# Hybrid pool and retention encoder on eight cores: first groups transposed on TensorE, last local means on GpSimd, output projection from its pool half

## The reference, cut to what matters

```python
mod = silu(c) @ ada_w + ada_b                      # conditioning
shift, scale, gate = split(mod, 3)
h = rms_norm(x, g_pre) * (1 + scale) + shift
u_pool, q, k, v, z = split(h @ w_in, ...)          # z is 2048 wide: z_pool | z_ret
y_pool = (window_mean(u_pool, w) - u_pool) @ pool_w * pool_scale   # w = 2, 4, 8, 16 by quarter of the width
y_ret = group_norm(retention_forward(q, k, v) + retention_backward(q, k, v))   # q, k rotated by position
out = (concat(y_pool, y_ret) * silu(z)) @ w_out
y = x + gate * rms_norm(out, g_post)
```

## Time and profile before

| what | value |
|---|---|
| median of 3 runs | 3066.83 us |
| profiled execution, device time | 3066.21 us |
| its span, slowest core (core 7) | 3064.6 us |
| spans of the cores | 3056.0 to 3064.6 us |
| busy, share of the span | PE 96%, DVE 78%, ACT 47%, POOL 41% |
| chain that ended last | PE 89%, DVE 4%, DMA 2%, issue 2% |

### The profile page before, as it was taken

One profiled execution on the slowest core, in us unless ns is written; L12 is line 12 of the kernel. 1 busy time (PEld: TensorE's weight loads), 2 busy tenths in 40 slices (PEclk: granted clock), 3 DMA queues, 4 the chain that ended last, 5 costly groups with the idle time before them and its releaser, 6 DMA issues.

```text
span 3064.6 us, 49885 instructions; the slowest of 8 cores (3056.0 to 3064.6 us)
## 1 busy us (share of the span) xinstructions
PE 2946.6 (96%) x17088; PEld 1475.1 (48%) x17088; DVE 2393.0 (78%) x2608; ACT 1431.7 (47%) x2381; POOL 1259.7 (41%) x968
## 2 busy tenths in 40 slices
PE   2799999999999999999799999999999999999998
PEld 1344444444444444444345555555555555555554
DVE  5488878888888878778777788777887777877774
ACT  5555556555556556553234434443444333443342
POOL 4444554554543333332134433443344433443343
PEclk9999999999999999999899999999999999999999
DMA  9966666666666655643868777777777778777774
GB/s 265 279 181 172 167 174 174 167 194 170 171 174 173 194 161 158 162 143 115 264 172 206 228 211 201 205 203 223 211 203 207 201 220 220 202 209 199 220 194 129
DMA packets 512857, 591.63 MB, mean 193 GB/s; under 512 B 329152, under 2 KB 353760, under 8 KB 505696
## 3 DMA queue, kind: packets, MB, share of 16 engines
q1 hardware_dynamic: 504352, 572.71, 66.2%
q0 software_dynamic: 3456, 10.49, 2.3%
q10 hardware_dynamic: 4800, 5.24, 0.8%
HBM read 305.70 MB, written 200.81 MB: 165 GB/s over the span
## 4 chain that ended last, share of the span: by engine, by line
PE 89%; DVE 4%; DMA 2%; issue 2%; ACT 1%; POOL 1%; ACTq 0%; SPq 0%; DVEq 0%; POOLq 0%
PE psum L848 59%; PE psum L1446 21%; PE psum L1379 4%; PE psum L1336 1%; PE psum L1412 1%; PE psum L948 1%; DMA krS<-kr 1%; ACT hT L831 1%; DMA stg<-wv 1%; ACTq L180 0%; DMA yT<-yr 0%; DVE kr L915 0%; DVE t L913 0%; DVE psum L914 0%; DVE SB L958 0%
## 5 line engine op out<-in xcount | busy, mean ns | idle before, releaser
L1386 POOL TENSOR_TENSOR rs<-st,mhalf 128x8 f32<-128x8 f32 x96 | 159.1, 1658 | 829.8 <-DVE st L1385 829.8
L920 POOL TENSOR_TENSOR kb<-kr,kd 128x1024 bf16<-128x1024 bf16 x94 | 233.9, 2488 | 456.0 <-DVE kr L915 431.4
L1446 PE MATMUL psum<-wo,yp 128*128 128x512 bf16 x1536 | 367.0, 382 | 9.8 <-DMA yT<-yr 9.6
L1446 PE MATMUL psum<-wo,yT 128*128 128x512 bf16 x1536 | 365.1, 381 | 0.0
L848 PE MATMUL psum<-hT,wu 128*128 128x512 bf16 x1536 | 350.3, 382 | 13.2 <-ACT hT L831 8.8
L848 PE MATMUL psum<-hT,wq 128*128 128x512 bf16 x1536 | 348.7, 380 | 3.8 <-ACT szp L991 3.0
L848 PE MATMUL psum<-wzr,hT 128*128 128x512 bf16 x1536 | 349.5, 381 | 0.0
L848 PE MATMUL psum<-hT,wzp 128*128 128x512 bf16 x1536 | 346.9, 379 | 0.0
L848 PE MATMUL psum<-wk,hT 128*128 128x512 bf16 x1472 | 332.7, 379 | 0.0
L848 PE MATMUL psum<-wv,hT 128*128 128x512 bf16 x1472 | 332.7, 379 | 0.0
L1420 ACT CAST fb<-SF 128x1024 bf16<-128x1024 f32 x94 | 98.2, 1045 | 345.6 <-DVE SF L1418 345.4
(11 more groups left out here) (189 smaller groups left out, 5316.3 us busy)
## 6 DMA issues: line engine op xcount, KB each, us to landing
xn<-x SPq DMA_DIRECT2D x191, 512.0 KB, 5.0
y<-xn SPq DMA_DIRECT2D x96, 512.0 KB, 2.8
krS<-kr SPq DMA_DIRECT2D x96, 256.0 KB, 2.3
hS<-hT SPq DMA_DIRECT2D x24, 1024.0 KB, 4.5
ypS<-yo SPq DMA_DIRECT2D x24, 1024.0 KB, 6.6
hT<-hS SPq DMA_DIRECT2D x24, 1024.0 KB, 7.4
vB<-vS SPq DMA_DIRECT2D x96, 256.0 KB, 3.6
QT<-qo SPq DMA_DIRECT2D x384, 64.0 KB, 2.4
```

What stands on the lines that cost most here:

```text
L920: pool(lambda e: e.tensor_tensor(out=h3(kb[:, :]), in0=h3(kr[:, :]), in1=bch(kd[:, 1, :]), op=ALU.mult), 2.3, r=[krb, kdb_], w=[kbb])
L1386: pool(lambda e: e.tensor_tensor(out=rs[:, :], in0=st[:, :], in1=mhalf[:, :], op=ALU.pow), 1.65, r=[stb, mhalfb], w=[rsb])
L1446: last = e.matmul(pp(p, half * 512, half * 512 + 512), l_, wo[:, ec, half * 512:half * 512 + 512], start=(ec == 0), stop=(ec == 15))
```

## The change

**Transposes.** The x tiles of groups 0 and 1 are no longer transposed by DMA. The new `front_pe` lets PE multiply the 32 blocks of 128x128 of a group with an identity matrix (idn, one DVE instruction) into PSUM, and ACT and DVE take them out of PSUM, four instructions of 128x512 each, with the scale and shift in the same instruction. For group 1 that stands between the third and the fourth u stage of group 0. A fourth xh tile is added for these two groups. The first three x tiles of group 2 are loaded before the loop of pass A instead of in its first step, and hT of group 1 is stored behind the last PE instruction of the start, as that of group 0 was.

**Last local means.** For the last group of pass A the adds of j = 1 and 2 and their products with silu(z) go to POOL; the order of j is 3, 1, 2, 0, all four before the first q. The loads of wq and wzr are held until the last product of the loop (yo_last). The gate z of chunk 1 comes before the first scores.

**Output projection.** Each `stage_out` runs both halves of the width with the pool half's eight blocks first, then both with the retention half's; only the second part waits for yT.

**Durations** that the scheduler is given change for loads of the start (fast 1.37 to 1.22), casts on POOL (1.9 to 1.1), the conditioning's products (1.3 to 0.4) and the two POOL instructions of `front_x` (0.3 and 0.55 to 0.8 each). One Sin now waits for the three Exp of the start.

```diff
+    (idn, idnb, _), = Area(gs_r.items[0][1].lo).alloc("idn", [128, 128], BF16)
+    xh0_r = Ring(list(xh_r.items) + Area(ag_r.items[0][1].lo).alloc("xh0", [128, 1024], BF16, 1))
...
+    dve(lambda e: e.tensor_single_scalar(out=idn[:, :], in_=dif[:, :], scalar=0.0, op=ALU.is_equal), 0.2, r=[difb], w=[idnb])
...
+        after=exps)
...
-        trT[k] += [dma(ht[:, :, i * 128:(i + 1) * 128], xh[:, :], xhk, r=[xhb], tr=True, late=late, q="act" if k == 0 else "sp", **({"w": [hb]} if n_ == 0 else {"a": [hb]}))]
+        trT[k] += [dma(ht[:, :, i * 128:(i + 1) * 128], xh[:, :], xhk, r=[xhb], tr=True, late=late, **({"w": [hb]} if n_ == 0 else {"a": [hb]}))]
...
+    def front_pe(k):
+
+        s, g = groupsA[k]
+        hTile[(s, g)] = ht, hb, hk = hA_r.next()
+        xs_ = [xhT.pop((k, 3 - i)) for i in range(4)]
+        out = []
+        for d2 in range(4):
+            p = sc.pair("px")
+
+            def f(e, d2=d2, p=p):
+                last = None
+                for x in range(2):
+                    for i in range(4):
+                        dc = 2 * d2 + x
+                        o_ = x * 512 + i * 128
+                        last = e.matmul(pp(p, o_, o_ + 128), xs_[i][0][:, dc * 128:(dc + 1) * 128], idn[:, :], start=True, stop=True)
+                return last
+            op("pe", f, mmc(8, 128), r=[x[1] for x in xs_] + [idnb], w=[p])
+            kw = {"w": [hb]} if d2 == 0 else {"a": [hb]}
+            dc = 2 * d2
+            o1 = act(lambda e, p=p, dc=dc: e.activation(out=ht[:, dc, :], in_=pp(p, 0, 512), func=AF.Identity,
+                                                        scale=gpr[:, dc, s:s + 1], bias=shf[:, dc, s:s + 1]), 0.65, r=[p, gprb, shfb], **kw)
+            o2 = dve(lambda e, p=p, dc=dc: e.tensor_scalar(out=ht[:, dc + 1, :], in0=pp(p, 512, 1024), scalar1=gpr[:, dc + 1, s:s + 1],
+                                                           scalar2=shf[:, dc + 1, s:s + 1], op0=ALU.mult, op1=ALU.add), 0.65,
+                     r=[p, gprb, shfb], a=[hb])
+            out.append([o1, o2])
+        return out
...
-        front_h(0, n_, 0.0)
     conditioning()
-    front_affine(0)
+    ev0 = front_pe(0)
...
-        front_h(1, n_, 0.0)
...
+        if j == 2:
+            front_pe(1)
     pend_kv = None
-    front_affine(1)
     last_pe = [o for o in sc.ops[-60:] if o.q == "pe"][-1:]
+    for n_ in range(3 if len(groupsA) > 2 else 0):
+        front_x(2, n_, after=[kc])
     store_h(0, last_pe)
+    store_h(1, last_pe)
...
-        for half in range(2):
...
+        for part in range(2):
+            for half in range(2):
+                def f(e, half=half, part=part):
+                    last = None
+                    for ec in range(8 * part, 8 * part + 8):
+                        l_ = yT[:, ec - 8, :] if part else yp[:, ec, :]
+                        last = e.matmul(pp(p, half * 512, half * 512 + 512), l_, wo[:, ec, half * 512:half * 512 + 512], start=(ec == 0), stop=(ec == 15))
+                    return last
+                op("pe", f, mmc(8, 512), r=[(ypb, yTb)[part]] + wos[2 * part:2 * part + 2],
+                   **({"w": [p]} if half == 0 and part == 0 else {"a": [p]}))
...
-    dma(fl(wq[:, :, :]), wqS.ap(), "wq", r=[dbuf("wqS")], w=[wqb])
+    dma(fl(wq[:, :, :]), wqS.ap(), "wq", r=[dbuf("wqS")], w=[wqb], after=[yo_last[0]])
...
-    for j in range(4):
+    pool_s = lambda fn, us, **k: pool(fn, 1.7 * us, **k)
+    for n_, j in enumerate((3, 1, 2, 0)):
         sz, szb = stage_zp(ps, pg, j)
-        stage_pool(ps, pg, j, sz, szb)
-        if j > 1:
-            stage_q(0, j - 2)
-    stage_q(0, 2)
+        stage_pool(ps, pg, j, sz, szb, dve if j == 3 else pool_s, (3, 0))
+    for j in range(3):
+        stage_q(0, j)
...
     stage_z(0, 0)
     stage_q(1, 0)
+    stage_z(1, 0)
     stage_scores(0, 0)
```

More of the change, by code:

```diff
@@ L612, in load @@
         bulk[0] += 1
-        return dma(out, in_, nm, w=w, after=after, rank=bulk[0], fast=1.37, nbytes=nbytes)
+        return dma(out, in_, nm, w=w, after=after, rank=bulk[0], fast=1.22, nbytes=nbytes)
     def cast(q, dst, src, r, w=(), a=()):
@@ L617, in cast @@
             return op("act", lambda e: e.copy(out=dst, in_=src), 1.05, r=r, w=w, a=a)
-        return op(q, lambda e: e.tensor_copy(out=dst, in_=src), 0.72 if q == "dve" else 1.9, r=r, w=w, a=a)
+        return op(q, lambda e: e.tensor_copy(out=dst, in_=src), 0.72 if q == "dve" else 1.1, r=r, w=w, a=a)
     load(sm[:, :], smalld.ap(), "sm", [smb])
@@ L821, in front_affine, with aff @@
         for d2 in range(4):
-            vec = k == 0 and d2 % 2 == 0
-            def aff(e, d2=d2, vec=vec):
+            def aff(e, d2=d2):
                 last = None
@@ L827, in aff @@
                     x_ = ht[:, dc, :]
[L828 to L831, removed]
-                return last
-            (dve if vec else act)(aff, 0.7 if vec else 1.25, r=[gprb, shfb], a=[hb], after=trT[k])
-        if k:
-            store_h(k)
+                    last = e.activation(out=x_, in_=x_, func=AF.Identity, scale=gpr[:, dc, s:s + 1], bias=shf[:, dc, s:s + 1])
+                return last
+            act(aff, 1.25, r=[gprb, shfb], a=[hb], after=trT[k])
+        store_h(k)
+    def front_pe(k):
[23 more added lines that the diff above has]
+        return out
     def store_h(k, after=()):
@@ L992, in stage_zp, with stage_pool @@
         return sz, szb
-    yoT = [None]
-    def stage_pool(s, g, j, sz, szb):
+    yoT, yo_last = [None], [None]
+    dve_ = dve
+    def stage_pool(s, g, j, sz, szb, dve=dve, ends=(0, 3)):
         u, ub = uT_.pop((s, g, j))
@@ L1027, in stage_pool @@
         v4 = lambda t: t.rearrange("p b (c t) -> p b c t", c=4)
-        (dve if j else pool)(lambda e: e.tensor_tensor(out=yo[:, :, 2 * j:2 * j + 2, :].rearrange("p c b t -> p b c t"), in0=v4(tok(m)),
+        yo_last[0] = (dve if j else pool)(lambda e: e.tensor_tensor(out=yo[:, :, 2 * j:2 * j + 2, :].rearrange("p c b t -> p b c t"), in0=v4(tok(m)),
                                                        in1=sz[:, :].rearrange("p (b c t) -> p b c t", b=2, c=4), op=ALU.mult),
-                             1.3 if j else 2.1, r=[mb, szb], **({"w": [yob]} if j == 0 else {"a": [yob]}))
-        if j == 3:
+                             1.3 if j else 2.1, r=[mb, szb], **({"w": [yob]} if j == ends[0] else {"a": [yob]}))
+        if j == ends[1]:
             dma(ypS[s].ap()[4 * g:4 * g + 4].rearrange("c p n -> p c n"),
@@ L1057, in f @@
                 return last
-            return op("pe", f, mmc(2, 512), r=[hb, Wp[half][d2]], **({"w": [ps[c]]} if half == 0 and d2 == 0 else {"a": [ps[c]]}))
+            first = name == "pv" and half == 0
+            return op("pe", f, mmc(2, 512), r=[Wp[half][d2]] + ([] if first else [hb]), after=ev0[d2] if first else (), **({"w": [ps[c]]} if half == 0 and d2 == 0 else {"a": [ps[c]]}))
         for d2 in range(4):
@@ L1224, in build_program @@
                 tgen += 1
-            if k == 1 and j == 0 and len(groupsA) > 2:
-                front_x(2, 0, after=pace)
-                front_x(2, 1, after=pace)
-                front_x(2, 2, after=pace)
             kx, jx = (k + 1, 3) if j == 0 else (k + 2, j - 1)
@@ L1440, in stage_out @@
         p = sc.pair("pout")
-        for half in range(2):
-            def f(e, half=half):
-                last = None
-                for ec in range(16):
-                    l_ = yp[:, ec, :] if ec < 8 else yT[:, ec - 8, :]
-                    last = e.matmul(pp(p, half * 512, half * 512 + 512), l_, wo[:, ec, half * 512:half * 512 + 512], start=(ec == 0), stop=(ec == 15))
-                return last
-            op("pe", f, mmc(16, 512), r=[ypb, yTb] + wos, **({"w": [p]} if half == 0 else {"a": [p]}))
+        for part in range(2):
[8 more added lines that the diff above has]
+                   **({"w": [p]} if half == 0 and part == 0 else {"a": [p]}))
         fs, fsb, _ = fs_r.next()
```

23 lines of the change are left out of this document (9 added, 14 removed).

## The result

The changed kernel takes 3031.3 us (median of four runs) where the kernel before takes 3067.2 beside it: a ratio of 0.9881, 95% interval 0.9858 to 0.9903, or 36 us less; 3027 was forecast. The profiled run of the changed kernel has a span of 3028.3 us, 36.3 less than before.

A forecast was written before the change was run, and what follows sets the result against it. It took PE's work to bound the two long stages and the DMA engines the start; -19 - 2.5 - 13 - 4.5 = -39 from 3066.2 gave 3027 us, range 3012 to 3051.

The forecast's parts named there:

- What bounds it: Two long stages bound by PE's work and unchanged; the gain lies in PE's idle 74.0, 22.0 and 15.3 us elsewhere.
- The start, -19: Start, bound by DMA engines: removing eight DMA transposes and group 1's wait for hT saves 19 us (9 to 24).
- the last wk cast comes about 15 us earlier: Start: without the DMA transposes the last wk cast moves from 87.48 to 72.5 us, and wuT with it.
- so that this costs nothing: Start: rotation table on POOL delays the last ada_w cast by 7.56 us, but gpr still precedes the last wv reduction.
- 4 us for ACT: Start: ACT's casts, held up 10.72 us by the issue of one transpose, come earlier; 4 us of it taken.
- 6.1 for hT: Start: PE's wait of 6.14 us for group 1's hT goes, as PE makes hT during u of group 0.
- Rival A: Start: transposes cost the DMA engines no more than loads; about -7 instead of -19, so 3039 us; chance 0.15.
- The 3.3 times of the prediction: Start, first 60 us: DMA transposes took 10.5 us per MB of the engines' time, plain loads 3.2.
- Group 2, -2.5: Group 2's first u in pass A: earlier x loads and transposes remove PE's 2.64 us wait for hT; -2.5 us.
- Pass B's beginning, -13: Where pass B begins: shorter waits give -8.8 us and less low clock -3.7, taken as -13 (4 to 18).
- QT moves little: Where pass B begins: QT lands about as before; z of chunk 1 fills 3.5 of the 7.14 us wait, 3.6 left.
- yT, -4.5: Last output stages: pool-half products cover four waits for yT, 6.4 us in all; -4.5 us (2.4 to 6.4).

The follow-up runs named there:

- the table alone: Changed kernel with one more dependence, putting group 1's rotation table on POOL behind the last ada_w cast: ratio 0.9843, span 3025.4 us.
- the copies: Two runs of the kernel before with its eight DMA transposes made plain DMA copies of the same 256 KB, in pieces of 256 bytes and 2 KB: 0.9986 and 0.9977.
- small copy: Kernel before with the eight DMA transposes of groups 0 and 1 made plain DMA copies in pieces of 256 bytes: ratio 0.9986, 4 us.
- large copies: Kernel before with the eight DMA transposes of groups 0 and 1 made plain DMA copies in pieces of 2 KB: ratio 0.9977, 7 us.

## Why the prediction was right, and where its reasons were not

- **What bounds it.** Right: the steady pass B moved by 0.5 us of 1420, pass A by 3.2 of 1326, 1.9 of it at its first u, and all the rest came from the three stages with gaps.
- **The start, -19.** Measured -12.1, or about -14 with the slow first u that the forecast counted here. The step that failed is "the last wk cast comes about 15 us earlier", at 72.5: it came 8.5 earlier, at 78.95. The new durations got no term; of the new order only POOL's table was priced, "so that this costs nothing", and the table alone is indeed little of it (gpr's last step ran at 48.34, inside the forecast's 44 to 50). But the order as a whole takes some 4 us back at that cast: it lies at 78.2 to 80.6 on the eight cores, and at 72.7 to 76.7 with the old durations. And with these, too, no core gains 15 there; they gain 4.9 to 13.2. The price was read off core 7, one of the two where the transposes took most of the DMA engines, and 4 us for ACT were added. The 19 us that the DMA path costs in the new order can't confirm the term of 19, as that order made the DMA path dearer. The reason holds at the weights, where the load on the DMA engines is most of the price, but by the copies that is 4 to 7 us of the kernel's time. What is left holds the DMA's latency and the pass on ACT behind it, which the forecast had only in its 6.1 for hT.
- **Rival A**, that nothing but group 1's wait would come back, is refuted by the 19 us: with the DMA path back the span is 3047.5 and u at 142.96, where it had 3033 to 3037 and 124 to 127. Of its rule in the Trainium skill, "Advanced Engine Details and Errata", X-Bar Transpose (TRN2): the shares disagree with it also against plain copies of the same pieces (9.8 to 18.5% against 7.7%), by 1.3 to 2.4 times from core to core. The 3.3 times of the prediction came from the dear end of the cores and from loads of far larger pieces.
- **Group 2, -2.5.** The wait went, as forecast, but little of it was kept: pass A gave some 1.3 us beside the first u, and a wait of 2.20 for kr stands at group 3's beginning.
- **Pass B's beginning, -13.** Measured -10.7. The wait for wq (2.17 for 2.5), the end of the waits for scm and yT, and a new wait of 2.1 on ACT's decays came as said. The step that failed is "QT moves little": z of chunk 1 filled 3.5 us, but QT's last DMAs took 10.7 us to land beside wo, dtot, afab and rT.
- **yT, -4.5.** The right mechanism, the term too small: -9.8. The waits of 6.4 went, and with them the low clock behind each, which I had counted in pass B's beginning but not here: PE was busy 77.10 us before and 72.92 after for the same products, at a granted clock of 0.93 and 0.97.
- The forecast of 3027 was thus near by luck, by errors of opposite sign: 5 too much in the start, 1 at group 2, 2 at pass B's beginning, 5 too little at the end.

## What to carry to other kernels

Before a DMA in a chain of work is replaced, price three things apart: its load on the DMA engines, its latency in the chain, and the pass over the tile that stands behind it. Here only the first was measured alone, at 4 to 7 us of the kernel's time. A table of durations for a scheduler is a change of its own: build it alone. Undo one edit at a time, and remember that it is undone in the new order of the queues: here the DMA path reached u of group 1 9.5 us later in the new order than in the old. When a wait falls, count the low clock behind it too, and ask which load has been moved in front of the next one.

## What was not expected of the hardware

ACT's long issue was not a matter of transposing. The third small copy held ACT's queue nearly as long as the transpose in the earlier trace rows (8.2 to 9.6 us on the eight cores, 9.3 to 12.5 for the transposes); the third large one did not. The first row is of the small copies (core 5), the second of the large ones (core 3):

```profile
18.01 8.41 ACTq L184 DMA_DIRECT2D hT<-xh  x1
```
```profile
15.10 0.47 ACTq L184 DMA_DIRECT2D hT<-xh  x1
```

And the transposes' share of the DMA engines differed between cores that do the same work, 9.8% on core 4 and 18.5% on core 2. The first u of group 1 differed too: core 0 of the kernel before reached it 6.4 us ahead of core 7:

```profile
127.10 3.15 PE L848 MATMUL psum<-hT,wu 128*128 128x512 bf16 x7 [5.97 <-ACT hT L831]
```

After the change all eight cores start that u between 120.5 and 121.9 us. That the transposes made the spread is not shown: core 4, with the least share, was among the late ones (130.92), and the large copies, which transpose nothing, spread from 119.5 to 124.1 on cores 0 to 3. The metric is the slowest core, so what varies between cores is paid at its worst.
